# Opening of a two-layer hybrid encoder: the first two conditioning matrices in column halves, and the first two up-product items begun on four k-tiles

## Chip, cores and metric

The kernel runs on one core of a Trainium2 chip. The metric is the device time of one execution in microseconds (us), the median of three timed executions: 2648.08 us before the change. TensorE is called PE below, VectorE DVE, ScalarE ACT, GpSimd POOL, and SyncE, which issues most transfers, SP.

## What is computed

Two layers (`DEPTH = 2`) over a sequence of 256 tokens and 1024 channels, all in float32. Each layer is a feed-forward block, a token mixer and a second feed-forward block, each fed by a modulated norm whose shift and scale come from a conditioning vector `c`. Only the start of the first feed-forward block bears on the change:

```python
c_act = jax.nn.silu(c)
mod = (c_act @ ada_w[l] + ada_b[l]).reshape(bsz, N_SUB, 3, D_MODEL)
h = rmsnorm(x, norm_w[l, 0]) * (1.0 + mod[:, 0, 1, None]) + mod[:, 0, 0, None]
g, u = jnp.split(h @ ffn_w13[l, 0], 2, axis=-1)      # D_FF = 2816
x = x + 0.5 * mod[:, 0, 2, None] * rmsnorm((silu(g) * u) @ ffn_w2[l, 0], norm_w[l, 1])
```

`ada_w[l]` holds nine 1024 x 1024 matrices. Number 0 gives the shift and number 1 the scale of the first norm, so `h`, and with it the whole kernel, has to wait for these two.

## The kernel before, in words

The channel axis is cut into `KT = 8` k-tiles of 128, the tokens into `TT = 2` tiles of 128. `hT[:, k, t*P:(t+1)*P]` is k-tile `k` of the modulated norm for token tile `t`, with channels on partitions. Each engine runs its own program in order and waits on semaphores.

**Transfers (SP).** SP issues into one queue: `x`, then the two conditioning matrices by rows (`conditioning`, four k-tiles of all 1024 columns in one transfer, the last four k-tiles of matrix 1 in two transfers), then the weights of items 0 and 1 of the up product. An item is 256 gate columns and 256 up columns, two transfers of 1 MB, into one of two ring slots (`up_weights`, L812). Item `j` with `j >= 2` is only issued when the product that read slot `j - 2` is done (`slot_free`). Behind them come 1 MB pieces of the further conditioning matrices (L777), three buffers, each refilled when DVE has summed it.

**Conditioning matrices 0 and 1.** The product with `c` is shared between two engines. PE multiplies k-tiles 3, 5 and 7 as one-column matmuls over 64-column blocks (`first_conditioning`, L1311 to L1323). DVE scales and adds k-tiles 0, 1, 2, 4 and 6 into one tile (`first_sum`), and PE adds that sum with a column of ones. DVE adds the bias and forms `modc`, the shift and scale by channel.

**The norm.** ACT squares `x`, POOL takes the power of the mean (`rstd`), DVE scales `x` (`normalise`), PE transposes 16 tiles into PSUM banks 4 to 7 (`turn_norm`) and turns the parameters (`turn_params`). DVE and ACT then apply `modc` while they copy k-tiles 4 to 7 and 0 to 3 to `hT` (`modulate`).

**The first up product.** Item 0 is made one token tile at a time (`open_by_token`: 64 matmuls with 128 moving columns), item 1 over both token tiles (`up`: 32 matmuls with 256 moving columns). An f32 matmul leaves two records in the trace. Items 2, 4, 6, 8 and 10 of the first block (`SEVEN`) are made by seven quarter products `m1, m2, m4, m6, m7, m5, m3` of 8 matmuls each (`up_seven`); `m6` needs sums of the weights that DVE makes once they have landed (`up_sums`, four operations). Between items DVE sums conditioning pieces. All matmuls are recorded under the helper's line L1230, all three-operand sums under L2511 and all two-operand ones under L2505.

Of the kernel before, what the change touches and what calls it, by code (L numbers as in the profile page):

```python
# [21 lines left out]
P = 128  # L22
D = 1024
# [194 lines left out]
def cond_count(l, k):  # L218

    return COND_ORDER.index((l, k)) + 1  # L220
# [128 lines left out]
def build(nc, a, out):  # L349
    with ExitStack() as ctx:  # L350
# [208 lines left out]
        ada_tail = signal("ada_tail", 0, 16)  # L559
        out_stored = signal("out_stored", 0, 16)  # L560
# [150 lines left out]

        def settle(eng):

            eng.sem_inc(settled, 1)
# [42 lines left out]
        def _(sp):  # L757
# [23 lines left out]
            def conditioning(l, k):  # L781

                src = row(a["ada_w"], l)[:, :, k * D:(k + 1) * D].rearrange("a (k p) n -> p (a k) n", p=P)
                for half in range(2):
                    kk = slice(half * KT // 2, (half + 1) * KT // 2)
                    if k == 1 and half:
                        sp.dma_start(adas[:, 1, 4:6, :], src[:, 4:6, :]).then_inc(ada_loaded[1][1].sem, 16)
                        sp.dma_start(adas[:, 1, 6:8, :], src[:, 6:8, :]).then_inc(ada_tail.sem, 16)
                    else:
                        sp.dma_start(adas[:, k % 2, kk, :], src[:, kk, :]).then_inc(ada_loaded[k % 2][half].sem, 16)  # L790

            def feed_forward(l, f):
# [9 lines left out]
                def up_weights(j):  # L802
# [6 lines left out]
                    elif l or f:  # L809
                        sp.wait_ge(*group_done(l, (group_of(IT_FFB) if f else 0) - 1 + j))  # L810
# [24 lines left out]
                up_weights(0)  # L835
                up_weights(1)
# [8 lines left out]
            for l in range(DEPTH):  # L845
                if l == 0:
                    conditioning(0, 0)
                    conditioning(0, 1)
# [106 lines left out]
        def _(pool):  # L955
# [272 lines left out]
        def _(pe):  # L1228
# [80 lines left out]
            def first_conditioning(k, pair):  # L1309

                for kt in PART_KT + (0,):  # L1311
                    if kt == 0:
                        pe.wait_ge(*ada_summed(0, k + 1))
                    elif k and kt == 7:
                        pe.wait_ge(*ada_tail(0, 1))
                    else:
                        pe.wait_ge(*ada_loaded[k][kt // 4](0, 1))
                    by = ccol[:, kt:kt + 1] if kt else ones[:, 0:1]
                    for m in range(KT):
                        for c in range(0, P, 64):  # L1320
                            ins = mm(ps[c:c + 64, 2 * pair, m:m + 1], adas[:, k, kt, m * P + c:m * P + c + 64], by,
                                     kt == PART_KT[0] and m == 0, kt == 0 and m == KT - 1)
# [2131 lines left out]
```

## Time and profile before

| what | before |
|---|---|
| timed executions, us | 2647.03, 2648.08, 2648.61 |
| profiled execution, us | 2643.59 |
| its span, first to last instruction, us | 2641.9 |
| PE busy | 2527.2 us, 96% of the span |
| DVE busy | 1817.5 us, 69% |
| ACT, POOL busy | 20%, 9% |
| mean granted TensorE clock | 0.994 |
| read from HBM | 422.88 MB |

The span is counted from the first to the last instruction of one profiled execution, 1.7 us less than that execution's own time. PE is busy nearly throughout; where it isn't, is the start: before 12 us of the span it has done one small transpose. A busy share says nothing of the clock at which PE ran: the granted clock, 1.00 for 2.4 GHz and 0.50 for 1.2 GHz, stands in a column of its own.

### The profile page before, as it was taken

Reading aid. Unit: us, or ns where it says so; the run is one execution under the profiler, and the core shown is the slowest. Engines: PE = TensorE matmul, PEld = TensorE weight load, DVE = VectorE, ACT = ScalarE, POOL = GpSimd, SP = SyncE. Lnnn points to the kernel's source line nnn. Section 1 sums busy time; section 2 is a strip of 40 time slices with the busy share of each in tenths; the row PEclk is TensorE's granted clock in tenths of the full one; section 3 lists DMA queues with packets and bytes.
Section 4 is the critical chain, followed back from the end, with each engine's and each line's share of the span. In section 5 each row is a group of like instructions: output and inputs, shape, how many; then the busy total and the mean of one; then the engine's idle time right before and its main releaser. Section 6 shows DMA issues by size and latency. Waiting matters only on the chain.

```text
span 2641.9 us, 69930 instructions
## 1 busy us (share of the span) xinstructions
PE 2527.2 (96%) x31413; PEld 1893.2 (72%) x31413; DVE 1817.5 (69%) x3017; ACT 516.6 (20%) x1053; POOL 242.4 (9%) x372
## 2 busy tenths in 40 slices
PE   7999999999999999999999999999999999999998
PEld 6984877877775455499579758787778745556993
DVE  4786455667785876479879865556787758664765
ACT  1000232212221332110010011322222223321000
POOL 6200101000001101010000010110010011010000
PEclk9999999999999999999999999999999999999999
DMA  9985433322235552398577654423222275435543
GB/s 362 323 298 176 136 114 104 118 86 94 94 109 198 177 192 96 127 314 282 197 255 276 223 173 142 157 86 104 100 89 86 95 242 171 172 112 178 197 160 127
DMA packets 239004, 445.34 MB, mean 169 GB/s; under 512 B 8920, under 2 KB 103702, under 8 KB 238704
## 3 DMA queue, kind: packets, MB, share of 16 engines
q1 hardware_dynamic: 224016, 395.60, 43.0%
q0 software_dynamic: 12960, 38.98, 4.6%
q8 instruction: 246, 4.03, 0.6%
q10 hardware_dynamic: 1728, 6.29, 0.6%
q14 instruction: 54, 0.44, 0.0%
HBM read 422.88 MB, written 17.96 MB: 167 GB/s over the span
## 4 chain that ended last, share of the span: by engine, by line
PE 72%; DVE 18%; DMA 3%; issue 3%; ACT 2%; SPq 1%; POOL 1%; DVEq 0%; POOLq 0%; ACTq 0%
PE ps L1230 71%; DVE scratch L2505 10%; DVE scratch L2511 3%; DMA ring<-in_ffn_w 2%; DVE scratch L2508 1%; DVE ring L2505 1%; DVE gbc L2511 1%; DMA scratch<-acs_scratch 1%; PE ps L1259 1%; DVE scratch L2937 1%; DVE x L2511 0%; DMA acs_scratch<-scratch 0%; ACT scratch L2149 0%; PE ps L1947 0%; DVE merged L2505 0%
## 5 line engine op out<-in xcount | busy, mean ns | idle before, releaser
L1230 PE MATMUL ps<-scratch 64*64 64x32 f32 (+6 forms) x15928 | 785.0, 245 | 62.2 <-DVE scratch L2505 27.6
L1230 PEld LDWEIGHTS ps<-scratch 64*64 64x64 f32 (+2 forms) x15928 | 635.3, 141 | 246.1 <-issue 116.3
L1230 PE MATMUL ps<-hT,ring 64*64 64x256 f32 (+3 forms) x8096 | 784.6, 356 | 9.5 <-issue 3.3
L1230 PEld LDWEIGHTS ps<-hT,ring 64*64 64x64 f32 (+2 forms) x8096 | 636.4, 155 | 89.5 <-issue 17.8
L1230 PE MATMUL ps<-ring,hT 64*64 64x256 f32 (+2 forms) x2816 | 425.4, 423 | 5.5 <-DVE scratch L2511 2.6
L2505 DVE TENSOR_TENSOR scratch<-scratch 128x256 f32<-128x256 f32 (+5 forms) x557 | 339.0, 609 | 108.7 <-ACTq L2313 31.8
L1230 PE MATMUL ps<-ring,scratch 128*128 128x512 f32 x864 | 394.1, 594 | 2.5 <-DVE scratch L2508 1.3
L1230 PEld LDWEIGHTS ps<-ring,hT 64*64 64x64 f32 (+1 forms) x2816 | 229.1, 150 | 142.8 <-issue 115.9
L1230 PEld LDWEIGHTS ps<-ring,scratch 128*128 128x128 f32 x864 | 158.3, 190 | 172.2 <-issue 166.6
L2505 DVE TENSOR_TENSOR scratch<-scratch,ps 128x512 f32<-128x512 f32 (+2 forms) x385 | 195.6, 508 | 116.3 <-PE ps L1230 89.7
L2511 DVE SCALAR_TENSOR_TENSOR scratch<-scratch,ccol 128x1024 f32<-128x1024 f32 x120 | 154.7, 1289 | 15.5 <-DMA scratch<-in_ada_w 11.4
L1230 PE MATMUL ps<-scratch,ring 128*128 128x128 f32 x1120 | 136.5, 275 | 0.0
L1230 PEld LDWEIGHTS ps<-scratch,ring 128*128 128x128 f32 x1120 | 130.7, 192 | 0.0
L2505 DVE TENSOR_TENSOR scratch<-ps,lvl 128x128 f32<-128x128 f32 (+1 forms) x224 | 73.8, 330 | 69.2 <-PE ps L1230 66.5
L2511 DVE SCALAR_TENSOR_TENSOR scratch<-ps,der,scratch 128x255 f32<-128x255 f32 (+1 forms) x112 | 54.0, 482 | 92.2 <-ACTq L2193 88.7
L2508 DVE TENSOR_SCALAR scratch<-scratch 128x64 f32<-128x64 f32 (+6 forms) x256 | 85.3, 333 | 37.4 <-ACTq L2479 14.0
L1027 POOL TENSOR_TENSOR stat<-stat,mhalf 128x1 f32<-128x1 f32 x24 | 15.1, 629 | 883.7 <-DVE stat L2508 883.7
L2505 DVE TENSOR_TENSOR scratch<-ring 128x1024 f32<-128x1024 f32 (+1 forms) x55 | 65.3, 1186 | 31.9 <-DMA ring<-in_ffn_w 30.6
L2263 ACT ACTIVATE scratch<-ps 128x512 f32<-128x512 f32 x48 | 26.5, 595 | 257.5 <-PE ps L1230 257.5
L2505 DVE TENSOR_TENSOR scratch<-ring,scratch 128x1024 f32<-128x1024 f32 (+1 forms) x59 | 70.1, 1189 | 2.0
L2505 DVE TENSOR_TENSOR ring<-ring 128x1024 f32<-128x1024 f32 (+1 forms) x59 | 70.1, 1189 | 2.0
L1230 PE MATMUL ps<-hT,scratch 128*128 128x128 f32 x560 | 68.2, 275 | 0.0
(248 smaller groups left out, 1759.9 us busy)
## 6 DMA issues: line engine op xcount, KB each, us to landing
ring<-in_w_in SPq DMA_DIRECT2D x56, 2048.0 KB, 8.9
ring<-in_ffn_w SPq DMA_DIRECT2D x88, 1024.0 KB, 7.7
scratch<-in_ada_w SPq DMA_DIRECT2D x66, 1024.0 KB, 10.2
ring<-in_ffn_w SPq DMA_DIRECT2D x80, 512.0 KB, 5.6
ring<-in_w_branch_mamba SPq DMA_DIRECT2D x8, 2048.0 KB, 8.0
scratch<-acs_scratch POOLq DMA_DIRECT2D x24, 512.0 KB, 6.2
scratch<-fill_scratch SPq DMA_DIRECT2D x16, 512.0 KB, 8.5
ring<-in_w_branch_rwkv SPq DMA_DIRECT2D x4, 2048.0 KB, 10.8
```

The lines of the kernel that those rows point to most:

```text
L1027: pool.tensor_tensor(stat[:, to + t:to + t + 1], stat[:, mean + t:mean + t + 1], mhalf[:, 0:1], ALU.pow).then_inc(rstd_ready.sem, 1)
L1230: return pe.matmul(o, lhsT, rhs, start=start, stop=stop)
L1259: ins = pe.transpose(ps[:, 4 + 2 * t + kt // 4, (kt % 4) * P:(kt % 4 + 1) * P], of[:, t, kt * P:(kt + 1) * P], ident[:, :])
L2263: act.activation(dst, ps[:, FILL_BANKS[r], :], ACT.Identity).then_inc(fill_evac.sem, 1)
L2505: return dve.tensor_tensor(o, i0, i1, op)
L2508: return dve.tensor_scalar(o, i0, s1, s2, op0, op1)
L2511: return dve.scalar_tensor_tensor(out=o, in0=i0, scalar=s, in1=i1, op0=op0, op1=op1)
L2937: own.step(dve.tensor_tensor_scan(gi.rearrange(f512), reset[:, :, :].rearrange("p a b -> p (a b)"), lwb.rearrange(f512), 0.0, ALU.mult, AL ...
```

## The change

The two matrices are loaded, summed and applied in column halves: `h = 0` are columns 0 to 511, which give channels of k-tiles 0 to 3, and `h = 1` the rest. Items 0 and 1 are loaded in halves of four k-tiles. PE then works in this order: conditioning half 0 of both matrices; the first four k-tiles of item 0, over both token tiles; matrix 0 half 1; three k-tiles of item 1; matrix 1 half 1; the fourth k-tile of item 1; and the last four k-tiles of items 0 and 1. ACT copies k-tiles 0 to 3 as soon as half 0 of `modc` is there, DVE k-tiles 4 to 7 after half 1. `cond_count` is moved by two, since four halves are counted in place of two matrices; the semaphores of the three pieces serve three of the new loads, so a piece's wait counts one more.

```diff
-    return COND_ORDER.index((l, k)) + 1
+    return COND_ORDER.index((l, k)) + 3
+
+
+def first_count(k, h):
+
+    return 1 + k + 2 * h
+
+
+def first_turns(kt, t):
+
+    return TT * (kt % (KT // 2)) + t + 1
...
+        def first_loaded(k, h, part):
+
+            if h == 0:
+                return ada_loaded[k][part](0, 1)
+            return (piece_loaded[0], ada_tail, piece_loaded[1], piece_loaded[2])[2 * k + part](0, 1)
...
-            def conditioning(l, k):
-
-                src = row(a["ada_w"], l)[:, :, k * D:(k + 1) * D].rearrange("a (k p) n -> p (a k) n", p=P)
-                for half in range(2):
-                    kk = slice(half * KT // 2, (half + 1) * KT // 2)
-                    if k == 1 and half:
-                        sp.dma_start(adas[:, 1, 4:6, :], src[:, 4:6, :]).then_inc(ada_loaded[1][1].sem, 16)
-                        sp.dma_start(adas[:, 1, 6:8, :], src[:, 6:8, :]).then_inc(ada_tail.sem, 16)
-                    else:
-                        sp.dma_start(adas[:, k % 2, kk, :], src[:, kk, :]).then_inc(ada_loaded[k % 2][half].sem, 16)
+            def first_weights(k, h):
+
+                src = row(a["ada_w"], 0)[:, :, k * D + 512 * h:k * D + 512 * h + 512].rearrange("a (k p) n -> p (a k) n", p=P)
+                for part in range(2):
+                    kk = slice(part * KT // 2, (part + 1) * KT // 2)
+                    sp.dma_start(adas[:, k, kk, 512 * h:512 * h + 512], src[:, kk, :]).then_inc(
+                        first_loaded(k, h, part)[0], 16)
+
+            def first_up(j, part, sem):
+
+                w13 = row(a["ffn_w13"], 0)[:, 0, :, :].rearrange("a (k p) (u n) -> p (a k) u n", p=P, u=2)
+                dst = ring[:, ffn_item(0, j) % 2, :].rearrange("p (k u n) -> p k u n", k=KT, u=2)
+                kk = slice(part * KT // 2, (part + 1) * KT // 2)
+                for u in range(2):
+                    sp.dma_start(dst[:, kk, u, :], w13[:, kk, u, j * 256:(j + 1) * 256]).then_inc(sem, 16)
+
+            def open_program():
+
+                for k in range(2):
+                    first_weights(k, 0)
+                sp.wait_ge(*x_loaded(0, 1))
+                first_up(0, 0, x_loaded.sem)
+                first_up(1, 0, first_up_loaded.sem)
+                for k in range(2):
+                    first_weights(k, 1)
+                for j in range(2):
+                    first_up(j, 1, slot_loaded[ffn_item(0, j) % 2].sem)
+                sp.wait_ge(*ada_summed(0, first_count(1, 1)))
...
-                up_weights(0)
-                up_weights(1)
+                if (l, f) == (0, 0):
+                    open_program()
+                else:
+                    up_weights(0)
+                    up_weights(1)
...
-                    pool.wait_ge(*ada_summed(0, 2))
+                    pool.wait_ge(*ada_summed(0, first_count(1, 1)))
...
-            def first_conditioning(k, pair):
-
+            def first_conditioning(k, h, bank):
+
+                half = KT // 2
                 for kt in PART_KT + (0,):
                     if kt == 0:
-                        pe.wait_ge(*ada_summed(0, k + 1))
-                    elif k and kt == 7:
-                        pe.wait_ge(*ada_tail(0, 1))
+                        pe.wait_ge(*ada_summed(0, first_count(k, h)))
                     else:
-                        pe.wait_ge(*ada_loaded[k][kt // 4](0, 1))
+                        pe.wait_ge(*first_loaded(k, h, kt // half))
                     by = ccol[:, kt:kt + 1] if kt else ones[:, 0:1]
-                    for m in range(KT):
+                    for m in range(half * h, half * h + half):
                         for c in range(0, P, 64):
-                            ins = mm(ps[c:c + 64, 2 * pair, m:m + 1], adas[:, k, kt, m * P + c:m * P + c + 64], by,
-                                     kt == PART_KT[0] and m == 0, kt == 0 and m == KT - 1)
+                            ins = mm(ps[c:c + 64, bank, m:m + 1], adas[:, k, kt, m * P + c:m * P + c + 64], by,
+                                     kt == PART_KT[0] and m == half * h, kt == 0 and m == half * h + half - 1)
...
+                def opening_half(j, part, ks, loaded=None):
+
+                    par = ffn_item(f, j) % 2
+                    pe.wait_ge(*(loaded or slot_loaded[par](l, 2)))
+                    w = ring[:, par, :].rearrange("p (k u n) -> p k u n", k=KT, u=2)
+                    for k in ks:
+                        pe.wait_ge(*(hT_dve if part else hT_act)(0, first_turns(k, 1)))
+                        for q, o in enumerate(up_banks(j)):
+                            ins = mm(o, w[:, k, q // 2, (q % 2) * P:(q % 2 + 1) * P], hT[:, k, :],
+                                     k == 0 and q % 2 == 0, k == KT - 1 and q % 2 == 1)
+                    return ins
+
+                if (l, f) == (0, 0):
+                    half = KT // 2
+                    opening_half(0, 0, range(half), x_loaded(0, 3))
+                    first_conditioning(0, 1, 4)
+                    opening_half(1, 0, range(half - 1), first_up_loaded(0, 2))
+                    first_conditioning(1, 1, 6)
+                    opening_half(1, 0, range(half - 1, half), first_up_loaded(0, 2))
+                    for j in range(2):
+                        opening_half(j, 1, range(half, KT)).then_inc(up_done.sem, 1)
+                        if j:
+                            beside(j)
+                elif f:
                     open_by_token(l, 3, *up_ready(0), up_done)
                 else:
                     open_by_token(l, 1, *up_ready(0), up_done)
-                for j in range(1, FJ):
+                for j in range(1 if l or f else 2, FJ):
...
-                    first_conditioning(0, 0)
+                    first_conditioning(0, 0, 0)
                     for t in range(TT):
                         turn_norm(0, 1, t)
                     turn_params(0, 3)
-                    first_conditioning(1, 1)
+                    first_conditioning(1, 0, 2)
...
-            act.wait_ge(*hT_dve(0, 1))
-            for t in range(TT):
-                modulate(0, 1, 0, t)
+            act.wait_ge(*cond_evac(0, first_count(1, 0)))
+            act.wait_ge(*xn_turned(0, TT))
+            for kt in range(KT // 2):
+                for t in range(TT):
+                    act.activation(hT[:, kt, t * P:(t + 1) * P], ps[:, 4 + 2 * t, kt * P:(kt + 1) * P], ACT.Identity,
+                                   scale=modc[:, 8 + kt:9 + kt], bias=modc[:, kt:1 + kt]).then_inc(hT_act.sem, 1)
...
+            def first_modulation(h, banks):
+
+                half = KT // 2
+                for k in range(2):
+                    dve.wait_ge(*cond_done(0, first_count(k, h)))
+                    part = modc[:, 8 * k + half * h:8 * k + half * h + half]
+                    at = half * h
+                    ins = tt(part, ps[:, banks[k], at:at + half], prm[:, C_ADAB + 8 * k + at:C_ADAB + 8 * k + at + half], ALU.add)
+                    if k:
+                        own.step(ins)
+                        ins = stt(part, part, 1.0, prm[:, C_NORM + at:C_NORM + at + half], ALU.add, ALU.mult)
+                    raised(ins, cond_evac(0, first_count(k, h)))
...
-                    first_sum(0)
+                    first_sum(0, 0)
                     for t in range(TT):
                         normalise(0, 1, 1, t)
-                    first_sum(1)
+                    first_sum(1, 0)
                     dve.wait_ge(*params_evac(0, 1))
-                    conditioning(0, 0, 0)
-                    conditioning(0, 1, 2)
-                    scale_weights(0)
-                    for t in range(TT):
-                        modulate(0, 1, 0, t)
+                    first_modulation(0, (0, 2))
+                    first_sum(0, 1)
+                    first_sum(1, 1)
+                    first_modulation(1, (4, 6))
+                    dve.wait_ge(*xn_turned(0, TT))
+                    for kt in range(KT // 2, KT):
+                        for t in range(TT):
+                            ins = ts(hT[:, kt, t * P:(t + 1) * P], ps[:, 5 + 2 * t, (kt % 4) * P:(kt % 4 + 1) * P],
+                                     modc[:, 8 + kt:9 + kt], modc[:, kt:1 + kt], ALU.mult, ALU.add)
+                            raised(ins, hT_dve(0, first_turns(kt, t)))
+                    dve.sem_inc(hT_ready.sem, 1)
```

How the change moves instructions on PE, at the program's start, before:

```order
L1230 MATMUL ps<-ccol,scratch 64x1 x48
L1230 MATMUL ps<-ones,scratch 64x1 x16
L1259 MATMUL ps<-ident,scratch 128x128 x16
L1290 MATMUL ps<-ident,prow 128x128 x4
L1230 MATMUL ps<-ccol,scratch 64x1 x48
L1230 MATMUL ps<-ones,scratch 64x1 x16
L1230 MATMUL ps<-hT,ring 128x128 x64
L1230 MATMUL ps<-hT,ring 128x256 x32
L1230 MATMUL ps<-hT,ring 128x128 x16
```

The rows on `ccol` and `ones` are the conditioning, 64 matmuls for a matrix; `ident` marks the transposes; the row of 64 is item 0, that of 32 item 1, that of 16 the first two quarters of item 2. The same place of the changed kernel:

```order
L1265 MATMUL ps<-ccol,scratch 64x1 x24
L1265 MATMUL ps<-ones,scratch 64x1 x8
L1294 MATMUL ps<-ident,scratch 128x128 x16
L1325 MATMUL ps<-ident,prow 128x128 x4
L1265 MATMUL ps<-ccol,scratch 64x1 x24
L1265 MATMUL ps<-ones,scratch 64x1 x8
L1265 MATMUL ps<-hT,ring 128x256 x16
L1265 MATMUL ps<-ccol,scratch 64x1 x24
L1265 MATMUL ps<-ones,scratch 64x1 x8
L1265 MATMUL ps<-hT,ring 128x256 x12
L1265 MATMUL ps<-ccol,scratch 64x1 x24
L1265 MATMUL ps<-ones,scratch 64x1 x8
```

Behind these stands one row of 36 matmuls 128x256 (the last k-tile of item 1's first half, then both second halves), and the 16 of item 2. Half of the conditioning has moved in among the up product, and the 64 matmuls of 128 moving columns have become 32 of 256.

On SP, which issues the transfers, the program's start before, and with what each waits for:

```order
L758 DMA x<-in_x 128x2x1024
L790 DMA scratch<-in_ada_w 128x4x1024 x3
L787 DMA scratch<-in_ada_w 128x2x1024
L788 DMA scratch<-in_ada_w 128x2x1024
L812 DMA ring<-in_ffn_w 128x8x256 x4
L777 DMA scratch<-in_ada_w 128x2x1024 x3
L812 DMA ring<-in_ffn_w 128x8x256 [waits up_done]
L812 DMA ring<-in_ffn_w 128x8x256
L777 DMA scratch<-in_ada_w 128x2x1024 [waits piece_summed] x2
```

And in the changed kernel:

```order
L775 DMA x<-in_x 128x2x1024
L803 DMA scratch<-in_ada_w 128x4x512 x4
L812 DMA ring<-in_ffn_w 128x4x256 [waits x_loaded]
L812 DMA ring<-in_ffn_w 128x4x256 x3
L803 DMA scratch<-in_ada_w 128x4x512 x4
L812 DMA ring<-in_ffn_w 128x4x256 x4
L794 DMA scratch<-in_ada_w 128x2x1024 [waits ada_summed]
L794 DMA scratch<-in_ada_w 128x2x1024 x2
L847 DMA ring<-in_ffn_w 128x8x256 [waits up_done]
L847 DMA ring<-in_ffn_w 128x8x256
L794 DMA scratch<-in_ada_w 128x2x1024 [waits piece_summed] x2
```

The same bytes are issued up to the row that waits for `up_done`, which is item 2; what is needed for k-tiles 0 to 3 comes ahead of the rest, and the first piece has a wait in front of it.

## Rows read from the trace of the kernel before

**Rows 1.** PE's waits from 0 to 190 us: engine, line, releaser, us, times, longest

```profile
PE ps L1230 <- DMA scratch<-in_ada_w: 8.6, 2, 5.0
...
PE ps L1230 <- DMA ring<-in_ffn_w: 2.7, 1, 2.7
```

**Rows 2.** PE's timeline, 10 to 35 us: start, us, operation

```profile
17.50 3.58 PE L1230 MATMUL ps<-ccol,scratch 128*64 128x1 f32 x64 [3.57 <-DMA scratch<-in_ada_w]
...
22.72 3.68 PE L1259 MATMUL ps<-ident,scratch 128*128 128x128 f32 x16
26.19 0.93 PE L1290 MATMUL ps<-ident,prow 128*128 128x128 f32 x4
27.05 3.04 PE L1230 MATMUL ps<-ccol,scratch 128*64 128x1 f32 x96
30.38 1.87 PE L1230 MATMUL ps<-ones,scratch 128*64 128x1 f32 x32 [0.29 <-DVE scratch L2511]
34.91 0.58 PE L1230 MATMUL ps<-hT,ring 128*128 128x128 f32 x1 [2.66 <-DMA ring<-in_ffn_w]
```

**Rows 3.** SP's timeline, 0 to 100 us

```profile
10.76 21.29 SPq L812 DMA_DIRECT2D ring<-in_ffn_w  x4
32.09 10.08 SPq L777 DMA_DIRECT2D scratch<-in_ada_w  x3
52.15 0.99 SPq L812 DMA_DIRECT2D ring<-in_ffn_w  x2
...
65.97 0.99 SPq L812 DMA_DIRECT2D ring<-in_ffn_w  x2
```

**Rows 4.** DVE's timeline, 11.9 to 62 us

```profile
12.01 0.83 DVE L2508 TENSOR_SCALAR scratch<-scratch,ccol 128x1024 f32<-128x1024 f32 x1 [1.76 <-DMA scratch<-in_ada_w]
...
20.19 1.54 DVE L2508 TENSOR_SCALAR scratch<-x,stat 128x1024 f32<-128x1024 f32 x2
...
32.37 0.17 DVE L2505 TENSOR_TENSOR modc<-ps,prm 128x8 f32<-128x8 f32 x1 [1.84 <-PE ps L1230]
...
61.64 1.22 DVE L2505 TENSOR_TENSOR scratch<-ring 128x1024 f32<-128x1024 f32 x1 [2.95 <-DMA ring<-in_ffn_w]
```

**Rows 5.** stretches: PE, PEld, DVE, ACT, POOL busy, clock, DMA share, GB/s

```profile
27.00:30.00 3.00, 3.00 (x98) 2.96 (x96) 1.59 (x2) 0.60 (x1) 0.00 (x0) 1.00 1.10 354
30.50:32.00 1.50, 1.50 (x30) 1.50 (x32) 0.03 (x1) 0.00 (x0) 1.38 (x2) 0.50 1.10 349
34.90:40.40 5.50, 5.49 (x25) 5.49 (x26) 5.00 (x12) 2.50 (x5) 4.76 (x12) 0.50 1.05 395
40.50:52.10 11.60, 11.60 (x105) 11.60 (x105) 0.00 (x0) 0.00 (x0) 10.83 (x13) 1.00 1.04 395
52.20:66.00 13.80, 13.80 (x67) 12.17 (x66) 9.95 (x9) 0.58 (x2) 12.55 (x20) 1.00 0.92 332
```

**Rows 6.** stretches elsewhere, same columns

```profile
439.80:443.30 3.50, 1.00 (x36) 0.97 (x37) 0.29 (x1) 2.92 (x5) 0.00 (x0) 1.00 0.38 150
443.30:446.70 3.40, 3.40 (x48) 2.72 (x44) 3.04 (x7) 0.00 (x0) 0.00 (x0) 0.50 0.02 5
106.00:109.00 3.00, 3.00 (x78) 2.66 (x77) 2.88 (x3) 0.00 (x0) 0.00 (x0) 1.00 1.01 403
```

**Rows 7.** PE's timeline further on: transposes, seven-product item 6

```profile
126.32 1.95 PE L1230 MATMUL ps<-scratch 128*128 128x128 f32 x16
...
257.46 1.04 PE L1259 MATMUL ps<-ident,scratch 128*128 128x128 f32 x8
```

**Rows 8.** POOL's and ACT's timeline, 12 to 35 us

```profile
12.95 2.94 POOL L1027 TENSOR_TENSOR stat<-stat,mhalf 128x1 f32<-128x1 f32 x2
...
33.22 2.90 ACT L2113 ACTIVATE hT<-ps,modc 128x128 f32<-128x128 f32 x8 [5.47 <-DVE hT L2508]
```

**Rows 9.** DVE's timeline, 100 to 200 us: end of item 6's weight sums

```profile
120.95 1.22 DVE L2505 TENSOR_TENSOR scratch<-ring,scratch 128x1024 f32<-128x1024 f32 x1
```

**Rows 10.** issue to landing of item 5's two transfers, issued at 94.0 and 94.4 us

```profile
DMA to landing us min/median/max: 5.6/6.8/8.1
```

More of the change, by code:

```diff
@@ L559, in build @@
         ada_tail = signal("ada_tail", 0, 16)
+        first_up_loaded = signal("first_up_loaded", 0, 16)
         out_stored = signal("out_stored", 0, 16)
@@ L833, in pieces_next @@
                         next(asked, None)
-                up_weights(0)
-                up_weights(1)
+                if (l, f) == (0, 0):
+                    open_program()
+                else:
+                    up_weights(0)
+                    up_weights(1)
                 pieces_next(PIECE_BUFS)
@@ L845, in _ @@
             for l in range(DEPTH):
-                if l == 0:
-                    conditioning(0, 0)
-                    conditioning(0, 1)
                 feed_forward(l, 0)
@@ L1435, in sums_ready @@
                     pe.wait_ge(*down_sum(l, down_sum_count(f, f"w{i}")))
-                if f:
+                def opening_half(j, part, ks, loaded=None):
[20 more added lines that the diff above has]
+                elif f:
                     open_by_token(l, 3, *up_ready(0), up_done)
@@ L2637, in conditioning_pieces @@
                         dve.wait_ge(*cond_done(0, count - 2))
-                    dve.wait_ge(*piece_loaded[n % PIECE_BUFS](0, n // PIECE_BUFS + 1))
+                    dve.wait_ge(*piece_loaded[n % PIECE_BUFS](0, n // PIECE_BUFS + 2))
                     for m in range(each):
@@ L2650, in conditioning_pieces, with first_sum @@
                     yield
-            def first_sum(k):
-                total = adas[:, k, 0, :]
+            def first_sum(k, h):
+                half, cols = KT // 2, slice(512 * h, 512 * h + 512)
+                total = adas[:, k, 0, cols]
                 for kt in (0, 1, 2, 4, 6):
-                    if kt in (0, 4):
-                        dve.wait_ge(*ada_loaded[k][kt // 4](0, 1))
-                    if k and kt == 6:
-                        dve.wait_ge(*ada_tail(0, 1))
+                    if kt in (0, half):
+                        dve.wait_ge(*first_loaded(k, h, kt // half))
                     if kt == 0:
@@ L2662, in first_sum @@
                     else:
-                        ins = stt(total, adas[:, k, kt, :], ccol[:, kt:kt + 1], total, ALU.mult, ALU.add)
+                        ins = stt(total, adas[:, k, kt, cols], ccol[:, kt:kt + 1], total, ALU.mult, ALU.add)
                     if kt < 6:
                         own.step(ins)
-                raised(ins, ada_summed(0, k + 1))
+                raised(ins, ada_summed(0, first_count(k, h)))
+            def first_modulation(h, banks):
[9 more added lines that the diff above has]
+                    raised(ins, cond_evac(0, first_count(k, h)))
             def conditioning(l, k, bank=4):
```

1 line of the change is left out of this document (removed).

## The prediction

> **What bounds the kernel now.** I began with the list of PE's waits over the first 190 us: two on the conditioning matrices, 8.6 us together, and one on the weights of item 0, 2.7 us [rows 1]. Behind 34.9 us the first 150 us show none. So what PE gains or loses before item 2 is what the whole kernel gains or loses, as long as it meets no later wait. The timeline of PE at the start [rows 2] shows what there is to win: its first dense work, item 0, begins at 34.91, when the transfer lands. SP issues the four transfers of items 0 and 1 from 10.76 and is held until 32.05 [rows 3]; the queue is full, and the share of the DMA engines is 1.04 to 1.10 in each of these stretches [rows 5]. The start is bound by bytes, and the change brings none of them fewer; it only needs 6 MB of them, not 11, before PE can start the up product.
>
> The table of stretches adds the clock [rows 5, 6]. It is 1.00 in 27 to 30, 0.50 in 30.5 to 32 and in 34.9 to 40.4, and 1.00 after that. The 1.00 of a stretch before 27 isn't to be believed: 16 transposes take 3.68 us from 22.72 [rows 2], 0.23 us each, where 8 of them take 1.04 later, 0.13 each [rows 7]. PE starts at the low level.
>
> **The start of the up product, step by step.** The first 2 MB of conditioning are there at 12.0, the next 2 MB at 17.5 [rows 2, 4], so 1 MB takes some 2.7 us. In the new order the column half of matrix 0 (2 MB) is there at 12.0, that of matrix 1 at 17.5, the first halves of items 0 and 1 at some 20 and 23, the other 4 MB at 34, the second halves at 36 to 39, or later where the bias rows share the engines.
>
> - Conditioning half 0 of matrix 0 is 64 records of one column, 3.6 us by the low-clock row of 64 [rows 2]; 3 of 4 parts can be done by 13.9 and the rest by 14.5. It isn't the limit.
> - The power is: POOL's two operations run from 12.95 to 15.89 [rows 8]; the first half of that, then 0.77 for one `normalise` [rows 4], lets PE transpose from 15.4. Its 16 transposes take 3.7 and the parameters 0.9 [rows 2]: 20.0.
> - Half 0 of matrix 1 is 64 records more, 3.6 us at the low clock: 23.6. DVE's two small operations (0.17 and a gap each [rows 4]) and ACT's first two copies (2.90 for 8 [rows 8]) put the first matmul at **24.9**, 10.0 us before 34.91.
>
> **What PE does from there.** Item 1 before is 66 records in 13.8 us at the full clock [rows 5], by its 64 true ones 0.216 us each. Both items are now 128 such records, 27.6 us. Before, they took 65.97 - 34.91 = 31.1 us (SP's two rows, at 52.15 and 65.97, are the ends of items 0 and 1 [rows 3]): item 0 by 128-column matmuls took 17.2, of which 5.6 at the low clock. The terms up to the end of item 0:
>
> - first half of item 0, 32 records: 6.9 us, and for the clock half of the 5.6 us that the dense start before took until it rose [rows 5], 2.8. End 34.6.
> - matrix 0 half 1, 64 one-column records. Warm, 96 took 3.04 us and cold, 32 took 1.87 [rows 2]: 2.0 or 3.7. Warm: 36.7. DVE has its sum by then: the data landed near 28.
> - 24 records 5.2, second stretch 2.0, 8 records 1.7, 32 records 6.9: **52.5** for item 0, and 6.9 more, **59.4**, for item 1.
>
> Before, these ends were 52.15 and 65.97. So item 0 ends no earlier, and item 1 ends 6.6 us earlier.
>
> **The new wait.** Item 2 is issued when item 0 is done. Before, that was at 52.15, and DVE, which waited for the landing, starts its sums at 61.64 [rows 3, 4], 9.5 us later, which hid behind item 1. The bytes ahead of it are the same now and the queue is full, so it lands at 61.6 plus the 0.4 by which it is issued later: with an empty queue two such transfers take 0.4 + 8.1 = 8.5 us at most [rows 10], which would be 61.0. I take **61.9**. PE is ready at 59.4 and waits 2.5 us. Item 2 thus starts at 61.9 and not at 65.97: **4.1 us earlier**.
>
> DVE's sums for item 2 take 5 us from the landing (four of 1.22 [rows 4]), and `m1`, `m2`, `m4` ahead of the quarter that needs them 3 x 1.8 [rows 7], so PE need not wait again. DVE is on its old clock while PE is 4.1 us ahead. The tightest place that I find behind is item 6: its sums end at 122.17 [rows 9] and PE comes to `m6` at 126.32 [rows 7], 4.15 us later; its weights are issued by PE's own progress and move with it in part. Nothing is lost there. In return POOL's bias rows, constants and the first pieces wait for the fourth sum, near 34.5 in place of 30.4; their readers come after 60 us and hide that. Without that cover it would be 4 us.
>
> Sum against the profiled execution: 2643.6 - 4.1 = 2639.5. That execution was 4.5 us below the median of the timed ones, and I carry the difference over: 2648.1 - 4.1 = **2644.0 us**.
>
> **What the clock can do.** The dips tell what comes before a fall: in 439.8 to 443.3 PE worked 1.00 of 3.50 us, and the next 3.4 us stood at 0.50. A stretch of one-column matmuls acts in the same way: PE was busy for 3.00 of 3.00 us from 27 on and the clock fell behind it [rows 5]. But 64 quick ones of 0.7 us among dense work left it at 1.00 [rows 6]. The new stretches of 2.0 us lie between the two. The page "TensorE: Matmul & The Clock Gate" of the Trainium skill, in its section on HAM oscillation, blames idle gaps of PE for the return to half rate; by it the clock would hold through the conditioning stretches, which have no idle, and the terms above stand. This trace disagrees on the stretch from 27 to 30.
>
> **The rivals.**
>
> 1. *The clock falls at the wait for item 2.* For: 2.5 us of idle is near what stood before the dip at 439.8. Against: PE is dense right before and behind. A fall costs from 1.7 us (half of 3.4 [rows 6]) to 2.8 (half of 5.6 [rows 5]). Time 2646.1.
> 2. *The clock falls at both conditioning stretches.* Each then costs 1.7 to 2.8 and one runs longer: 4 to 7 us, item 0 ends at 56.5 to 59.5, item 2 lands 8.5 later, 65.0 to 68.0. That is from 1.0 faster to 2.0 slower, and with a third fall at the wait 4 slower: **slower than before**, 2650.1 at the middle of the upper half. It turns to the slow side when item 0 ends after 57.5. For: the stretch of 3.0 us before; against: the new ones are 2.0 and each has 5 us or more of dense work ahead.
> 3. *Item 2 lands sooner or the start is cleaner.* If the clock is up from the transposes on, item 0 ends near 49.7, and the landing is bound by the queue alone, perhaps 60.5: 5.5 faster, 2642.6.
> 4. *The second halves come late.* The bias rows are replicated reads that run beside them; before, they ran beside item 1. PE needs item 0's second half at 45.6, some 7 us after it is due. Only a lag above that costs, and then one for one; I give 2 us, 2646.0.
> 5. *The gain is lost again* between items 3 and 10, where the DMA engines are near full: the 4.1 us would shrink to what slack lets through. No change then, 2648.
>
> **How the numbers follow.** 0.2%, 5.3 us, is about what a measurement of this kernel can tell from no change. Chances: my forecast 0.42 (its own range 2643 to 2645.5), rival 1 0.18, rival 2 0.12, rival 3 0.16, rival 4 0.05, rival 5 0.07. From 2642 to 2649 lies all but rival 2's upper half and the end of rival 3. Faster by over 5.3 us is most of rival 3, 0.15; slower by over 5.3 us needs all falls together and a late start, 0.04; within, 0.81.
>
> **What the profile will show.** Right: the first 256-column matmul near 25; item 0's end near 52.5 and item 1's near 59.4, with PE then waiting on item 2's transfer until about 61.9; a clock that rises near 30 and stays up. Wrong: a granted clock of 0.50 anywhere between 35 and 60, a first matmul after 27, a wait of PE on `slot_loaded` at item 0's second half, or new waits of PE behind 66 us.

## The result, and the profile after

| | before | changed |
|---|---|---|
| timed together, median of 7 executions each, us | 2647.03 (2643.36 to 2649.14) | 2654.36 (2649.13 to 2659.33) |
| profiled execution's span, us | 2641.9 | 2657.6 |
| mean granted TensorE clock in it | 0.994 | 0.992 |

The ratio is 1.0029, 95% interval 1.0015 to 1.0042: **0.3% slower**, 7.3 us, where 4 us faster was forecast. The profiled execution of the changed kernel was the slowest of its seven, so the pair of traces, 15.7 us apart, overstates the loss. The experiments were timed later in three groups, in which the kernel before had medians of 2642.96, 2642.12 and 2643.88 us; so ratios are compared between groups, and times only within one.

The start first. PE's waits from 0 to 190 us after the change (columns as in [rows 1]):

```profile
PE ps L1265 <- DMA ring<-in_ffn_w: 5.2, 1, 5.2
PE ps L1265 <- DMA scratch<-in_ada_w: 4.2, 2, 2.3
PE ps L1265 <- ACT hT L2237: 1.5, 1, 1.5
```

The two waits on the conditioning matrices have shrunk from 8.6 to 4.2 us [rows 1]. The one on an item's weights has grown from 2.7 to 5.2, and PE's timeline shows that it now stands ahead of item 2:

```profile
14.81 3.67 PE L1294 MATMUL ps<-ident,scratch 128*128 128x128 f32 x16
...
19.27 1.73 PE L1265 MATMUL ps<-ccol,scratch 128*64 128x1 f32 x48
...
22.93 8.83 PE L1265 MATMUL ps<-hT,ring 128*128 128x256 f32 x32 [1.46 <-ACT hT L2237]
31.69 1.57 PE L1265 MATMUL ps<-ccol,scratch 128*64 128x1 f32 x48
...
33.66 5.45 PE L1265 MATMUL ps<-hT,ring 128*128 128x256 f32 x24
39.03 1.57 PE L1265 MATMUL ps<-ccol,scratch 128*64 128x1 f32 x48
...
41.00 15.81 PE L1265 MATMUL ps<-hT,ring 128*128 128x256 f32 x72
62.01 6.42 PE L1265 MATMUL ps<-hT,ring 128*128 128x128 f32 x32 [5.20 <-DMA ring<-in_ffn_w]
...
78.92 1.46 PE L1265 MATMUL ps<-hT,ring 128*128 128x256 f32 x6
```

The up product begins at 22.93, not 34.91 [rows 2], and the second halves of items 0 and 1 end at 56.8. Then PE stands for 5.2 us, and item 2's first 32 records take 6.42 us. SP's timeline says why item 2 is late:

```profile
24.16 9.11 SPq L812 DMA_DIRECT2D ring<-in_ffn_w  x4
37.61 1.40 SPq L794 DMA_DIRECT2D scratch<-in_ada_w  x3
49.93 1.78 SPq L847 DMA_DIRECT2D ring<-in_ffn_w  x2
...
58.29 5.52 SPq L847 DMA_DIRECT2D ring<-in_ffn_w  x2
```

Item 2 is issued at 49.93, when item 0 is done, and stands behind three conditioning pieces that were issued from 37.61 on. It lands at 62.0, 12.1 us after its issue. The stretches, with the granted clock in the eighth column (columns as in [rows 5]):

```profile
19.70:23.10 3.40, 1.94 (x61) 1.88 (x60) 0.51 (x4) 1.39 (x5) 0.00 (x0) 1.00 1.10 351
23.10:26.50 3.40, 3.40 (x9) 2.69 (x9) 0.00 (x0) 3.07 (x7) 0.00 (x0) 0.50 1.06 386
26.50:60.60 34.10, 30.30 (x249) 26.26 (x247) 21.62 (x34) 1.19 (x2) 20.59 (x34) 1.00 1.06 383
60.60:67.40 6.80, 5.39 (x25) 5.40 (x26) 5.21 (x5) 0.38 (x1) 6.34 (x8) 0.50 1.04 390
67.50:190.00 122.50, 122.50 (x996) 112.59 (x996) 96.33 (x97) 6.44 (x12) 17.94 (x40) 1.00 0.91 322
```

The clock stood at 2.4 GHz (1.00) from 26.5 through both conditioning stretches, and at 1.2 GHz (0.50) from 60.6, while PE waited for item 2, to 67.4. Item 3 starts at 78.92. Before, it started at 80.00, by the same view:

```profile
80.00 1.24 PE L1230 MATMUL ps<-hT,ring 128*128 128x256 f32 x5
```

So 1.1 us of lead is left, and it lasts until the down product, the one with `ffn_w2` that follows the up product. There PE waits 1.83 us for DVE (before 0.70, start 193.80) and is level with before:

```profile
193.85 3.67 PE L1265 MATMUL ps<-scratch 128*128 128x512 f32 x8 [1.83 <-DVE scratch L2565]
```

The opening thus gave nothing in this execution, and it cost nothing. The 15.7 us all lie behind 194 us, where the diff changes no line, and nearly all of them in the mixers of the two layers. Part of them is the clock: 0.002 less in the mean over 2650 us is, as an estimate, 5 us. Most of the rest are longer pauses of PE. One kind of pause the profile calls "issue", which means that it finds nothing that PE waited for. Their sum over the whole span, before and after, grows by 4.2 us:

```profile
PE ps L1230 <- issue: 24.3, 19, 2.5
```

```profile
PE ps L1265 <- issue: 28.5, 20, 2.6
```

One such place in the trace after, and a queue that was at work in it (the profile's view of the DMA queues, from 761.1 to 762.2 us):

```profile
758.83 2.30 PE L1265 MATMUL ps<-scratch 64*64 64x32 f32 x75
763.56 0.80 PE L1265 MATMUL ps<-scratch 64*64 64x64 f32 x17 [2.44 <-issue]
```

```profile
q8 instruction: 1, 0.02, 5.9%
```

At the corresponding place before, the pause comes at other matmuls and is shorter:

```profile
756.47 1.56 PE L1230 MATMUL ps<-scratch 64*64 64x64 f32 x32
759.24 0.56 PE L1230 MATMUL ps<-scratch 64*64 64x64 f32 x20 [1.21 <-issue]
```

The page of the changed kernel gives this queue's total over the span:

```profile
PE 2535.2 (95%) x31349; PEld 1896.1 (71%) x31349; DVE 1821.1 (69%) x3030; ACT 516.4 (19%) x1053; POOL 240.6 (9%) x372
...
q8 instruction: 246, 4.03, 0.6%
```

PE's 62,698 records (matmuls and weight loads, twice 31,349) come to 255 for each of the 246 packets, and a packet carries 16 KB. I read from this that the queue brings code to PE in blocks of 256 instructions; the other queue of this kind has 54 packets, far too few. An f32 matmul leaves four records (two of PE, two of PEld), so it is four instructions. The change puts 32 matmuls of 256 columns in place of 64 of 128 and adds four waits: **124 instructions fewer**, and every block behind them ends at another place of the program.

### The profile page after: what moved, and what is told of

It reads as the page before. It is cut to its first block, busy times and chain, and to the rows that moved or that the text cites. A ratio compares the mean times of both kernels' runs of the same rounds, so it can differ in the third digit from the quotient of the medians.

```text
span 2657.6 us, 69830 instructions
## 1 busy us (share of the span) xinstructions
PE 2535.2 (95%) x31349; PEld 1896.1 (71%) x31349; DVE 1821.1 (69%) x3030; ACT 516.4 (19%) x1053; POOL 240.6 (9%) x372
## 4 chain that ended last, share of the span: by engine, by line
PE 69%; DVE 20%; DMA 5%; issue 3%; ACT 2%; POOL 1%; SPq 0%; DVEq 0%; POOLq 0%; ACTq 0%
PE ps L1265 67%; DVE scratch L2565 10%; DVE scratch L2571 4%; DMA ring<-in_ffn_w 3%; DVE scratch L2568 2%; DVE ring L2565 1%; DVE gbc L2571 1%; PE ps L1294 1%; DVE scratch L3015 1%; DMA scratch<-acs_scratch 1%; DMA acs_scratch<-scratch 0%; DVE x L2571 0%; ACT scratch L2390 0%; ACT scratch L2388 0%; DMA scratch<-in_ada_w 0%
## 5 line engine op out<-in xcount | busy, mean ns | idle before, releaser
L1265 PE MATMUL ps<-hT,ring 64*64 64x256 f32 (+2 forms) x8032 | 787.8, 358 | 12.4 <-DMA ring<-in_ffn_w 5.2
L1265 PEld LDWEIGHTS ps<-hT,ring 64*64 64x64 f32 (+1 forms) x8032 | 634.8, 155 | 94.9 <-issue 16.9
L2565 DVE TENSOR_TENSOR scratch<-scratch 128x256 f32<-128x256 f32 (+5 forms) x557 | 339.0, 609 | 111.3 <-ACTq L2373 31.7
L2571 DVE SCALAR_TENSOR_TENSOR scratch<-scratch,ccol 128x1024 f32<-128x1024 f32 (+1 forms) x128 | 156.9, 1226 | 14.3 <-DMA scratch<-in_ada_w 9.9
L2323 ACT ACTIVATE scratch<-ps 128x512 f32<-128x512 f32 x48 | 26.5, 595 | 257.2 <-PE ps L1265 257.2
```

The source lines that it names most:

```text
L1265: return pe.matmul(o, lhsT, rhs, start=start, stop=stop)
L2323: act.activation(dst, ps[:, FILL_BANKS[r], :], ACT.Identity).then_inc(fill_evac.sem, 1)
L2565: return dve.tensor_tensor(o, i0, i1, op)
L2571: return dve.scalar_tensor_tensor(out=o, in0=i0, scalar=s, in1=i1, op0=op0, op1=op1)
```

## The experiments

Two theories. *Layout* (L in the expectations): the loss is not of the opening; it comes from where the code blocks end behind it. *Opening* (O): the new order itself does it, through the wait for item 2, the clock or the transfers. The extra matmuls below, where nothing else is said, stand ahead of everything, while PE waits for the first matrices, and their result is not used. Kernels of one group (e1 to e4, e5 to e8, e9 to e12) were timed side by side, each with kernel before.

**Layout against opening (e1 to e4).** e1 is the changed kernel once more.

> The changed kernel once more, on one chip with the padded ones. Theory L (layout): the changed kernel has 124 instructions fewer on PE than before (32 matmuls fewer at four instructions each, four waits more), so every later PE instruction sits elsewhere in the 16 KB blocks in which instructions are fetched, and PE's stops at fetches in the mixer of both layers, 1 to 2.7 us each, fall in worse places. Theory O (opening): what is lost is lost in the first 200 us. Both expect this run some 7 us (5 to 9) above the kernel before; its profile shows the first feed-forward block ending as early as before, within 1.5 us.

Ratio 1.0025 (1.0013 to 1.0036): the loss is there again.

e2 puts the layout of before back (lines with `+` are added to the changed kernel):

```diff
+            for _ in range(31):
+                mm(ps[0:32, 7, 0:1], ident[:, 0:32], ones[:, 0:1])
             pe.wait_ge(*c_step(0, 3))
```

> The changed kernel with 31 one-column matmuls of 32 columns on constants (124 instructions), made while PE waits for the first conditioning weights, result unused: all later PE instructions sit where they sat before the change. Theory L expects 5 to 8 us less than the changed kernel, the kernel before within 2 us. Theory O expects the same time as the changed kernel, within 1.5 us, or up to 1 us more for the extra work.

Ratio 0.9996 (0.9983 to 1.0009): 31 matmuls that compute nothing take the loss away, 6.5 us between the medians of e1 and e2. e3 is the kernel before with 33 such matmuls, which gives it the layout of the changed one.

> The kernel before with 33 such unused matmuls (132 instructions) at the same place, where PE waits for its first weights for 5 us: later PE instructions sit as in the changed kernel, modulo 256 instructions (16 KB). Theory L expects 5 to 8 us more than the kernel before. Theory O expects the kernel before within 1 us.

Ratio 1.0030 (1.0016 to 1.0043). The old opening in the new layout is as slow as the changed kernel (5.0 us between the medians); Opening falls as the cause of the loss. That the 33 matmuls themselves cost the time is ruled out by e12 below, where 64 cost nothing measurable. The traces show the same pause at the same matmuls in e1 and in e3:

```profile
496.50 1.42 PE L1265 MATMUL ps<-scratch 64*64 64x256 f32 x29 [1.26 <-issue]
```

```profile
496.98 1.42 PE L1230 MATMUL ps<-scratch 64*64 64x256 f32 x29 [1.49 <-issue]
```

The changed kernel's own trace has it too (498.70, 1.55 us), and e10 below (490.68, 1.36 us). Before and e2 have none there; their block ends a few matmuls further on, and the pause is shorter, 0.71 us before and 0.63 in e2:

```profile
493.51 0.51 PE L1265 MATMUL ps<-scratch 64*64 64x64 f32 x10 [0.63 <-issue]
```

A pause can also have a cost behind it. Some 6 us later PE waits for DVE in e1, and in e3 and e10 alike (0.74 us each), where before runs the same 20 matmuls without a wait:

```profile
502.37 0.56 PE L1265 MATMUL ps<-scratch 64*64 64x64 f32 x20 [0.74 <-DVE scratch L2568]
```

```profile
501.08 0.56 PE L1230 MATMUL ps<-scratch 64*64 64x64 f32 x20
```

The places follow the layout to the record. Counted back from PE's last matmul record (two to a matmul, so a shift of one stands for two instructions), "issue" pauses end 28014, 26608 and 25331 records before the end in the kernel before, in e2, e5 and e6, and 28080, 26674 and 25269 before the end in the changed kernel, e1, e3 and e10. The first of them is at 27984 in e4, at 28030 in e8, at 28046 in e7 and at 27998 in e11: 30 less, 16 more, 32 more and 16 less, as the numbers of added instructions say. 28080 is 28014 less 62, for the change's 124 instructions, and plus 128, for one block.

e4 moves the changed kernel by 16 matmuls, a quarter of a block.

> The changed kernel with 16 such unused matmuls (64 instructions), a quarter of a fetch block. Theory L expects another time than both e1 and e2, anywhere between 2645 and 2658, since other places stop. Theory O expects e1's time within 1.5 us.

Ratio 1.0019 (1.0006 to 1.0032): a third layout, nearly as slow.

**Other layouts (e7, e8, e12).** e7 and e8 are e2 with 47 and 39 matmuls in place of 31; e12 is before with 64, one whole block, put ahead of the wait for `c`.

> After with 47 one-column matmuls ahead of everything: the code behind lies 64 instructions (a quarter of a fetched block) further on than before the change; e4 was a quarter block to the other side of the layout of before, e1 half a block. Layout theory: the time depends on where the blocks' ends fall, so anything from 2636 to 2652 is possible here; the opening is the same as in e2 within 1.5 us. If the layout of before is merely one of several that are alike, this is 2642 to 2644. If the time falls off with the distance from the old layout, it is near e4's, ratio 1.002.

> After with 39 one-column matmuls ahead of everything: the code behind lies 32 instructions (an eighth of a fetched block) further on than before the change. Layout theory: between e2 (0.9996) and e7, each stop of TensorE for code moved by a few matmuls. If the stops depend on how wide the matmuls are that run while a block is fetched, some of the 19 to 23 stops change length and the sum is within 2 us of e2's. Rival: layouts differ only in units of something larger, then it is e2's time.

> Before, with 64 one-column matmuls (256 instructions, one whole fetched block) ahead of everything, done while TensorE waits for c and the first matrices. If it is the place within a block of 256 instructions that counts: ratio 1.000, stops for code as long as before's. If each added instruction shifts the stops for good, or the sum of code counts: slower, 1.001 to 1.003 as with 33 (e3_before_pad33).

Measured: e7 1.0023 (1.0012 to 1.0035), e8 0.9999 (0.9987 to 1.0012), e12 1.0003 (0.9991 to 1.0015). So the place within a block counts, not the number of instructions ahead; an eighth of a block was free, a quarter cost 0.2%. What Layout expected of e4 and e7 was wide (2645 to 2658 and 2636 to 2652): it says that the time may change, not to which side.

To see where that time sits I added up, from the one trace of each kernel, PE's pauses of more than 0.6 us behind 200 us, measured from matmul start to matmul start, and set apart those that end within 1.6 us after a packet of the code queue has landed. These stretches cover 15% of the span, so some pauses fall into them by chance:

| layout against before | kernels | pauses behind a packet, us (number) | other pauses, us |
|---|---|---|---|
| the same | e2, e12 | 30.2 (22), 26.5 (19) | 72.3, 73.6 |
| the same | e5, e6, e9 | 36.2 (24), 34.6 (23), 30.8 (21) | 66.5, 65.7, 69.2 |
| +32 and -32 instructions | e8, e11 | 33.0 (22), 34.8 (25) | 72.7, 67.5 |
| +64 | e7 | 41.8 (28) | 70.6 |
| -60 | e4 | 46.9 (35) | 62.8 |
| -124, that of the change | e1, e3, e10 | 42.7 (32), 39.7 (28), 43.3 (32) | 66.4, 68.4, 65.4 |

In the table the cheap layouts (that of before, or up to 32 instructions off) have 19 to 25 pauses at a packet, the costly ones (-60, +64, -124) 28 to 35, and some 10 us more in them: 41.9 on average for that of the change, 31.7 for that of before. The other pauses show no such step: 62.8 to 70.6 us in the costly layouts, 65.7 to 73.6 in the others. Both columns together come to 108.7 and 101.1 us, and the 7.5 us between them are what the ratios say. The profiled executions of before and of the changed kernel, taken earlier, stand 7 and 6 us above their groups, at 38.4 (28 pauses) and 48.1 (32), with the same 10 us between them.

Most of the step is not in the pauses called "issue". Of those, 13 to 17 (22 to 27 us) end behind a packet in the cheap layouts and 14 to 18 (25 to 32 us) in the costly ones. The pauses behind a packet that the profile puts down to DVE are 4 to 11 us in the cheap layouts and 14 to 19 in the costly ones. Whether PE waits there for code on top of DVE, or for a DVE that an earlier pause made late, as at 502.37 in e1, these traces don't tell apart. Nor does the sum follow single executions: e10's profiled one has 9 us more behind packets than e6's and is 1.4 us shorter, at a clock of 0.997 against 0.993. That the layout costs the time is shown by the timed runs; where it sits is read from averages.

The page "Runtime: NRT & Kernel Launch" of the Trainium skill, in the section on instruction fetch mechanics, says that code is streamed in blocks of 256 instructions, with which these traces agree, and that this is hidden by the rate at which instructions are issued. It isn't hidden throughout here: the "issue" pauses that end behind a packet come to 22 to 32 us in each trace, about 1% of the time.

**What the opening itself is worth (e5, e6).** Both keep the 31 extra matmuls' worth of instructions, and with them the layout of before. e5 takes 10 of them as wide ones behind item 1:

```diff
                         if j:
                             beside(j)
+                    for _ in range(10):
+                        mm(ps[:, 7, 0:S], ident[:, :], hT[:, 0, :])
```

> After, with 31 more f32 matmuls on TensorE as in e2_after_pad31, so that the code behind lies as before the change; but 21 of them are one-column matmuls ahead of everything and 10 are 256-column matmuls into a free bank, put between the end of item 1 and the wait for item 2. They compute nothing that is used. They fill some 4.3 us of the 5 us in which TensorE otherwise idles for item 2's weights. If the idle is what makes the clock fall at 61 to 63 us: the clock stays at 1.00 from 26 on, item 2's first 32 records take 3.6 to 4.0 us and not 5.5 to 6.7, and item 3 starts near 76.5 (77.86 in e2, 79.37 in e4); time 1 to 2.7 us below e2's 2642.7, that is a ratio of 0.999. If the clock falls anyway (one-column stretches before it): item 3 at 77.9 to 79.4 and the time of e2.

Ratio 0.9982 (0.9974 to 0.9991). PE's timeline and the clock behind it:

```profile
56.48 4.48 PE L1265 MATMUL ps<-hT,ident 128*128 128x256 f32 x20
61.99 3.84 PE L1265 MATMUL ps<-hT,ring 128*128 128x128 f32 x32 [1.03 <-DMA ring<-in_ffn_w]
```

```profile
62.00:66.00 4.00, 4.00 (x35) 4.00 (x36) 3.86 (x3) 0.38 (x1) 3.73 (x4) 1.00 1.03 399
```

Item 2 starts when it did, at 61.99, but runs at 1.00 and takes 3.84 us, not 6.42. Item 3 starts at 76.33, where e2 has 77.86. So the idle brought the clock down. The fall cost 2.6 us in the changed kernel's own trace, where it lasted 6.9 us (6.42 against 3.84), and 1.6 in e2, where it lasted 3.4 (5.47). That is less than the 0.14%, 3.7 us, between the ratios of e5 and e2, whose intervals overlap. e6 lets item 2 go ahead of the third piece:

```diff
-                pieces_next(PIECE_BUFS)
+                held = 1 if (l, f) == (0, 0) else 0
+                pieces_next(PIECE_BUFS - held)
                 for j in range(2, FJ):
                     up_weights(j)
+                    if j == 2:
+                        pieces_next(held)
```

> After with the 31 one-column matmuls of e2_after_pad31, and the third conditioning piece issued behind item 2's weights, not ahead of them. If item 2 is bound by the bytes ahead of it: it lands 2.7 us earlier, near 59.3, TensorE's wait shrinks from 3.9 to 5.2 us to 1.5 to 2.5, and if the clock holds over that, item 3 starts at 73.5 to 74.5, 3.5 us before e2; if it falls, 75.5 to 76.5. DVE's pieces have enough buffered to be no later. The time is then 2 to 4 us below e2, ratio 0.998 to 0.9985, if the lead survives the rest of the block. Rival: the rest of the first block is bound by the transfers and DVE's sums (its weights and pieces are back to back), so the down product still starts at 191.7 to 193.9 and the time is that of e2.

Ratio 0.9976 (0.9965 to 0.9987), median 2637.65 us against 2642.12 of before. PE's timeline:

```profile
59.35 5.46 PE L1268 MATMUL ps<-hT,ring 128*128 128x128 f32 x32 [2.82 <-DMA ring<-in_ffn_w]
...
75.31 4.91 PE L1268 MATMUL ps<-hT,ring 128*128 128x256 f32 x22
...
189.11 3.67 PE L1268 MATMUL ps<-scratch 128*128 128x512 f32 x8 [0.70 <-DVE scratch L2570]
```

It lands 2.6 us sooner, as 1 MB less ahead of it should give. The clock falls all the same, after 2.82 us of idle. The lead is there at the down product too: 189.11, where before had 193.80 and e12, the same opening as before, 192.81. So the rest of the block does not bound it.

**Together (e9 to e11).** e9 is e6 with 5 wide matmuls in the wait, e10 is e6 without extra matmuls, e11 has 23.

> e6_piece_behind with 5 of the 31 extra matmuls made 256 columns wide and put between item 1 and the wait for item 2, as in e5_after_filled: they fill 2.2 of the 2.8 us of idle. If e5's reading is right the clock stays at 1.00 from 26 to 190 us, item 2's first 32 records take 3.7 us in place of 5.46, and item 3 starts near 73.6 (75.31 in e6); time 1.7 us below e6's 2637.65 at most, ratio 0.997. If the down product is bound by transfers and sums by then (start at 189.11 in e6), the 1.7 us are lost there and the ratio is e6's 0.9976.

> e6_piece_behind without the 31 extra one-column matmuls: the code behind lies as in the changed kernel. If layout and opening are independent, the layout costs 0.25 to 0.3% and the opening gives 0.24% back: ratio 1.000 to 1.001, 6 to 8 us above e6. If the gain of e6 had come from something else than the opening, it could be as fast as e6.

> e6_piece_behind with 23 extra one-column matmuls and not 31: the code behind lies 32 instructions (an eighth of a fetched block) ahead of that of before the change, where e8 had it 32 behind and came out alike. If the layouts within an eighth of the old one are alike: ratio 0.997 to 0.998. If the time rises towards e4's side (64 ahead, 1.0019): ratio 0.9985 to 0.9995.

Measured: e9 0.9979 (0.9968 to 0.9991), e10 1.0006 (0.9991 to 1.0021), e11 0.9981 (0.9966 to 0.9996). In e9 the clock holds and item 3 starts at 73.92, but the down product gives some back:

```profile
59.39 3.84 PE L1268 MATMUL ps<-hT,ring 128*128 128x128 f32 x32 [0.57 <-DMA ring<-in_ffn_w]
...
73.92 6.42 PE L1268 MATMUL ps<-hT,ring 128*128 128x256 f32 x29
...
188.42 3.67 PE L1268 MATMUL ps<-scratch 128*128 128x512 f32 x8 [1.36 <-DVE scratch L2572]
```

Of 1.4 us more lead at item 3 than in e6, 0.7 is left, too little for the times to tell. e10 against e6 is 0.30% apart, as e1 against e2 (0.29%) and e3 against before (0.30%): the layout's cost doesn't depend on the opening. Four versions beat both kernels: e5, and e6, e9 and e11, which are at 0.21% less than before in the mean of their three ratios; all four are alike within their intervals.

e11's trace shows a second kind of start. Its up product begins at 24.81 and its clock is up from 30.9 on; e4 is like it (24.34, up from 27.2). In the other traces of the changed order it begins at 22.15 to 23.18, after a stretch of 3.4 us at 1.00 that starts at 17.9 to 19.7. In e11 item 2 is only issued at 53.15 and lands at 61.33, not at 59.35; PE waits 1.31 us for it. Its clock held and item 3 started at 76.89.

## Why the prediction was wrong, point by point

- **"Sum against the profiled execution", 2643.6 - 4.1.** This is the step that failed. It held everything behind the opening to be worth what it was before. The layout of the code added 0.29 to 0.30% (e1 against e2, e3 against before, e10 against e6), near 8 us by the ratios and 5 to 6.5 by the medians, more than the gain forecast. No term and no rival spoke of it, though the rows on `issue` and on the code queue stood in the profile of before, and the number of instructions that the change drops can be read off the program. Of the 11.4 us between -4.1 and +7.3 it is some 8. Most of the remainder is the opening's own term, 4.1 us. With the layout put back it was worth 1 us by e2's time, whose interval reaches from 4.5 us faster to 2.4 slower, and 0.6 us at item 3 by the traces. The fall of the clock, which was priced as a rival and left out of the sum, took it.
- **The start of the up product, 24.9.** It was 22.93. The clock was at 1.00 from 19.7 to 23.1, so the 64 records of matrix 1 took 2.2 us (48 in 1.73) and not 3.6. It then fell for 3.4 us. In e4 and e11, where the 48 took 2.73, the start was at 24.34 and 24.81: the forecast's case exists, but in two of eleven traces.
- **Item 0's end 52.5, item 1's 59.4.** They were 49.93 and 56.8, 2.6 us earlier, because of that start and of what was left of the low clock in the first half, which ended at 31.7, not 34.6. Stretches and dense parts were within 0.3 us of the forecast: 2.0, 5.45, 2.0, 15.8 us. That is the start of rival 3 (item 0 at 49.7). Its landing at 60.5 did not come.
- **"The new wait", item 2 at 61.9.** It landed at 62.0. The reason given, that the bytes ahead set it, held: with 1 MB less ahead it landed at 59.35 (e6), and with item 0 done 2.6 us earlier than forecast it came no sooner. The 0.4 us added for a later issue had no part in it, so the last few tenths are luck. In e11, with less ahead and issued at 53.15, it landed 8.2 us later: there the issue set the landing, the other bound that the prediction named (8.5 us). What failed is the other side: PE was ready at 56.8, and the wait was 5.2 us, not 2.5.
- **Rival 1, the clock falls at that wait.** It happened in each run of the changed order with a wait of 2.8 us or more there (2.82 in e6 is the shortest) and in none with less (e11 1.31, e5 1.03, e9 0.57). Its price was 1.6 to 2.8 us (item 2's first 32 records took 5.45 to 6.66 where it fell, 3.84 where it held), against the 1.7 to 2.8 given. It had 0.18 and should have been the forecast, above all once the wait is 5.2. Here the page "TensorE: Matmul & The Clock Gate" of the Trainium skill, in its section on HAM oscillation, blames idle gaps, and the trace agrees.
- **Rivals 2 and 4.** Rival 2 is refuted: 26.5 to 60.6 stood at 1.00. So is rival 4: PE ran from 41.00 to 56.8 without a wait for the second halves.
- **Item 2 "4.1 us earlier".** 62.01 against 65.97 [rows 3] is 4.0. The clock took 2.6 of it and the rest of item 2 0.3, so 1.1 was left at item 3. And 80.00 was a late one: e12 and e3, with the old opening, have 78.99 and 78.83. The six traces with the transfers as in the change and nothing put into the wait (the changed kernel, e1, e2, e4, e7, e8) have 77.86 to 79.37, 78.65 on average against 79.27 for the three of the old opening. So the opening is worth some 0.6 us, and e2's and e8's times say as little (0.9996 and 0.9999).
- **"Nothing is lost there", rival 5.** This held for the most part. The changed kernel's own trace lost its 1.1 us to a DVE wait of 1.83 us, but e2 kept all of the same lead against e12 (1.1 us at item 3 and at the down product, 191.68 against 192.81). Of larger leads against e12, e5 kept 2.4 of 2.7, e6 all 3.7 and e9 4.4 of 5.1.

Left open: why a block is late at some matmuls and in time at others was not tested, and so neither was which layout is best. Six offsets in a block of 256 were tried. The 14 traces together give a strong hint. Behind 200 us they hold 3282 code packets, and 212 have an "issue" pause behind them. For 208 of these 212, the other queues took more than 45% of the DMA engines' time from 1 us before the packet's start to 1 us after it. That was so for 1006 packets in all; of the other 2276, 4 had a pause. Where that share was over 80%, 178 of 328 packets had a pause if PE ran more than 12 matmul records per us in the 2 us before, and none of 341 if it ran fewer. So the pauses come where many small matmuls meet full DMA engines. That the full engines cause them is argued from this, not shown: no run took the other transfers away.

That more dips of the clock follow in a costly layout, as the first pair of traces suggests (0.994 and 0.992), is not borne out: the profiled e10, in the costly layout, had 0.997 and e6, in the other, 0.993.

## What to carry to other kernels

A change that adds or drops instructions on an engine with tens of thousands of them moves the code blocks of everything behind. Before a difference of a few tenths of a per cent is put down to the change, time it once more with as many idle instructions added as bring the layout back, and give the kernel before the new layout too. If a trace shows pauses called "issue", look whether a code packet lands just ahead of them, and what the DMA engines are doing there. When a change makes an engine ready sooner, move the transfer it will wait for next by as much, or the wait comes back with a fall of the clock on top. A second profile of the kernel before shows how firm a time is on which a sum of a few us rests.

## What the runs showed of the hardware

- PE's code comes in packets of 16 KB, 246 or 247 in these kernels. In each trace PE has 13 to 18 "issue" pauses of 1.5 to 1.9 us on average behind them, 22 to 32 us in all or about 1% of the time. Shifting the program by 60 to 124 instructions moved the kernel by 0.2 to 0.3% (e4, e7, e3); shifting it by 32, or by 256, did not measurably (e8, e12).
- These pauses stand where the other queues load the DMA engines: 208 of 212 at a share above 45%, 4 at less, though 2276 of 3282 packets came at less.
- The granted clock went to 0.50 after an idle of 2.8 us between dense work (e6), and didn't when 2.2 us of 2.8 were filled (e9). Two stretches of 2.0 us of one-column matmuls among dense work left it at 1.00 in the changed kernel.
